# Value products of a pair's two heads issued together, alternating by key chunk, in a two-block attention network

## The reference

```python
# stick-breaking, 16 heads of 64 (first block, second layer)
z = q @ k.T * scale; suffix = reversed exclusive cumsum of log_sigmoid(-z)
wts = where(key < query, exp(log_sigmoid(z) + suffix), 0);  out = wts @ v
# second block, first layer: 8 global heads (2 key/value heads), 8 window heads (|rel| <= 128, bias, sink)
p = softmax(q @ k.T * scale [+ bias]);                      out = p @ v
# second block, second layer: 16 neighbourhood heads (8 rows x 16 columns of a 64-wide grid, bias)
p = softmax(where(colmask, q @ k.T * scale + bias, -inf));  out = p @ v
# both layers of the second block: 4 memory heads of 128 over 256 memory keys
```

## Time and profile before

| | |
|---|---|
| median of three runs | 2174.17 us |
| the profiled execution, its time | 2174.26 us |
| its span, first to last instruction | 2172.3 us |
| TensorE matmuls busy | 2086.6 us, 96% of the span |
| VectorE, ScalarE, GpSimd busy | 1155.4, 806.0, 131.6 us |
| mean granted TensorE clock | 0.981 |
| data moved | 173.78 MB, 80 GB/s on the mean |

### The profile page before, as it was taken

One profiled execution on the slowest core, in us unless ns is written; L12 is line 12 of the kernel. 1 busy time (PEld: TensorE's weight loads), 2 busy tenths in 40 slices (PEclk: granted clock), 3 DMA queues, 4 the chain that ended last, 5 costly groups with the idle time before them and its releaser, 6 DMA issues.

```text
span 2172.3 us, 26051 instructions
## 1 busy us (share of the span) xinstructions
PE 2086.6 (96%) x8940; PEld 1552.7 (71%) x8940; DVE 1155.4 (53%) x1991; ACT 806.0 (37%) x1402; POOL 131.6 (6%) x223
## 2 busy tenths in 40 slices
PE   6997999999999998999999998999998999999987
PEld 6875888888876665888888874555576866666766
DVE  6576544434555565544434555556744466666543
ACT  5365322222334444332222333534433333334331
POOL 1000000000000000000000000000003033332000
PEclk9999999999999999999999997999999999999998
DMA  6422223223321111222322320011122222222221
GB/s 217 145 79 67 90 96 104 97 89 96 106 69 58 49 48 39 89 97 97 111 82 97 104 71 20 29 64 47 56 74 74 85 68 69 69 68 56 83 73 68
DMA packets 48347, 173.78 MB, mean 80 GB/s; under 512 B 7345, under 2 KB 9409, under 8 KB 48017
## 3 DMA queue, kind: packets, MB, share of 16 engines
q1 hardware_dynamic: 41184, 160.45, 22.5%
q0 software_dynamic: 7088, 12.37, 2.3%
HBM read 168.58 MB, written 4.21 MB: 80 GB/s over the span
## 4 chain that ended last, share of the span: by engine, by line
PE 89%; DVE 6%; ACT 3%; issue 2%; DMA 1%; POOL 0%; DVEq 0%; ACTq 0%; SPq 0%; POOLq 0%
PE ps L366 24%; PE ps L368 23%; PE ps L367 23%; PE ps L458 7%; PE ps L486 7%; PE ps L466 3%; PE ps L544 1%; DVE Wl L1054 1%; ACT Wh L718 1%; DVE stat L1183 1%; DMA nmask<-in_nmask 1%; PE ps L435 0%; DVE scr L1180 0%; PE ps L401 0%; DMA Wr<-in_w 0%
## 5 line engine op out<-in xcount | busy, mean ns | idle before, releaser
L366 PE MATMUL ps<-Hh,Wh 128*128 128x512 f32 x1568 | 642.1, 410 | 0.0
L368 PE MATMUL ps<-Hh,Wl 128*128 128x512 f32 x1568 | 614.1, 392 | 0.0
L367 PE MATMUL ps<-Hl,Wh 128*128 128x512 f32 x1568 | 613.7, 391 | 0.0
L718 ACT ACTIVATE Wh<-Wr 128x1024 fp32r<-128x1024 f32 (+2 forms) x276 | 308.8, 1119 | 708.9 <-PE ps L368 696.2
L1054 DVE TENSOR_TENSOR Wl<-Wr,Wh 128x1024 fp32r<-128x1024 f32 (+2 forms) x276 | 359.3, 1302 | 240.1 <-ACT Wh L718 240.0
L366 PEld LDWEIGHTS ps<-Hh,Wh 128*128 128x128 f32 x1568 | 295.3, 188 | 142.2 <-issue 85.3
L368 PEld LDWEIGHTS ps<-Hh,Wl 128*128 128x128 f32 x1568 | 295.3, 188 | 64.5
L367 PEld LDWEIGHTS ps<-Hl,Wh 128*128 128x128 f32 x1568 | 295.7, 189 | 55.6 <-issue 0.7
L366 PE MATMUL ps<-Yh,Wh 128*128 128x512 f32 (+1 forms) x800 | 304.2, 380 | 30.9 <-DVE Yl L1084 16.5
L367 PE MATMUL ps<-Yl,Wh 128*128 128x512 f32 (+1 forms) x800 | 300.2, 375 | 0.0
L368 PE MATMUL ps<-Yh,Wl 128*128 128x512 f32 (+1 forms) x800 | 299.8, 375 | 0.0
(11 more groups left out here) (173 smaller groups left out, 1559.4 us busy)
## 6 DMA issues: line engine op xcount, KB each, us to landing
Wr<-in_w SPq DMA_DIRECT2D x228, 512.0 KB, 3.4
Wr<-in_w SPq DMA_DIRECT2D x32, 768.0 KB, 4.2
Wr<-in_w SPq DMA_DIRECT2D x16, 640.0 KB, 3.9
scr<-in_rpb POOLq DMA_DIRECT2D x128, 24.0 KB, 2.0
X<-in_x SPq DMA_DIRECT2D x1, 2048.0 KB, 13.6
scr<-in_wri POOLq DMA_DIRECT2D x4, 512.0 KB, 3.9
out_t<-X SPq DMA_DIRECT2D x8, 256.0 KB, 2.1
scr<-d_rel POOLq DMA_DIRECT2D x8, 192.0 KB, 3.3
```

What stands on the lines that cost most here:

```text
L366: pe.matmul(bank[:, 0:n], hi, rh[:, k, :], start=(k == 0), stop=False)
L367: pe.matmul(bank[:, 0:n], hi, rl[:, k, :], start=False, stop=False)
L368: return pe.matmul(bank[:, 0:n], lo, rh[:, k, :], start=False, stop=(k == kc - 1))
L718: act.activation(Wh[:, slot, 0:kc * P], Wr[:, slot, 0:kc * P], ACT.Copy).then_inc(w_hi, 1)
```

## The change

`values` is left to the memory heads. A new `values_pair` takes both heads of a pair: it goes over the key chunks, and within a chunk over the two heads, so that the products alternate between the two halves of `ps[6]`. It is called once for each pair, where head 1's visit stood; the call at step 6 is gone. It waits once for `t_pt`, `v_ok` and `yt_ok`. `t_av` is counted up by each head's last product, as before. In the gqa part the wait for `xf_ok` (the final norm of the first block has read `ps[6]`) moves from step 6 of pair 0 to step 2 of pair 1. No other engine's program changes.

```diff
--- before.py
+++ after.py
@@ -466,25 +466,30 @@
                     mm = pe.transpose(ps[4 + j % 2][:, n * P:(n + 1) * P], Pb[:, j % 4, n * P:(n + 1) * P], ident[:, :])
                 mm.then_inc(t_t, 1)
 
-            def values(kind, g, par, h, o, grp, v_need):
+            def values(g, par, h, o):
 
                 pe.wait_ge(t_pt, g + 1)
-                wait(pe, v_ok, v_need)
-                if h == 0 or kind == MEMA:
-                    wait(pe, yt_ok, o)
-                cs = range(2) if kind == MEMA else range(4)
-                for c in cs:
+                wait(pe, yt_ok, o)
+                m = 2 * par + h
+                for c in range(2):
+                    mm = pe.matmul(ps[6][:, :], memVa[:, c, m * P:(m + 1) * P], PT[:, h, c * S:(c + 1) * S],
+                                   start=(c == 0), stop=(c == 1), skip_group_check=True)
+                mm.then_inc(t_av, 1)
+
+            def values_pair(kind, g, par, o, grp, v_need):
+
+                pe.wait_ge(t_pt, g + 1)
+                pe.wait_ge(v_ok, v_need)
+                wait(pe, yt_ok, o)
+                for c in range(4):
                     q0, q1 = query_range(kind, c)
-                    rhs = PT[:, h, c * S + q0:c * S + q1]
-                    if kind == MEMA:
-                        m = 2 * par + h
-                        lhs, out = memVa[:, c, m * P:(m + 1) * P], ps[6][:, :]
-                    else:
+                    for h in range(2):
                         vb, off = {STICK: (par, h), NBR: (par, h), GQA: (0, grp), WIN: (1, grp)}[kind]
-                        lhs = Vn[:, vb, c * P + 64 * off:c * P + 64 * off + 64]
-                        out = ps[6][64 * h:64 * h + 64, q0:q1]
-                    mm = pe.matmul(out, lhs, rhs, start=(c == 0), stop=(c == cs[-1]), skip_group_check=True)
-                mm.then_inc(t_av, 1)
+                        mm = pe.matmul(ps[6][64 * h:64 * h + 64, q0:q1],
+                                       Vn[:, vb, c * P + 64 * off:c * P + 64 * off + 64], PT[:, h, c * S + q0:c * S + q1],
+                                       start=(c == 0), stop=(c == 3), skip_group_check=True)
+                        if c == 3:
+                            mm.then_inc(t_av, 1)
 
             def pump(j, nu, u0, t0, slot0):
 
@@ -580,9 +585,7 @@
                         if not (first and j < 2):
                             turn(kind, g - 2, (j - 2) % 8)
                         if j == 2 and not first:
-                            values(kind, g - 3, 1 - par, 1, i + (o0 - 1), 0, i + nv0)
-                        if j == 6:
-                            values(kind, g - 3, par, 0, i + o0, 0, i + (nv0 + 1))
+                            values_pair(kind, g - 3, 1 - par, i + (o0 - 1), 0, i + nv0)
                 pair(0, 0, True, False)
                 with pe.Fori(0, 3) as it:
                     pair(2 * it + 1, 1, False, False)
@@ -591,7 +594,7 @@
                 g = g0 + 64
                 turn(kind, g - 2, 6)
                 turn(kind, g - 1, 7)
-                values(kind, g - 1, 1, 1, o0 + 7, 0, nv0 + 8)
+                values_pair(kind, g - 1, 1, o0 + 7, 0, nv0 + 8)
 
             def mem_heads(seg, name, first_q):
                 plain_units(name, first_q, 4)
@@ -608,10 +611,10 @@
                             turn(MEMA, g - 2, (j - 2) % 8)
                         if j in (2, 6) and g - 3 >= g0:
                             hd = 2 * i + (j - 6) // 4
-                            values(MEMA, g - 3, hd // 2, hd % 2, OUT0[seg] + hd, 0, 0)
+                            values(g - 3, hd // 2, hd % 2, OUT0[seg] + hd)
                 turn(MEMA, g0 + 14, 6)
                 turn(MEMA, g0 + 15, 7)
-                values(MEMA, g0 + 15, 1, 1, OUT0[seg] + 3, 0, 0)
+                values(g0 + 15, 1, 1, OUT0[seg] + 3)
 
             pairs8("stick", STICK, "sb_qkv", 3, 8)
             out_proj("sb_out", KD, Y0["sb"])
@@ -689,15 +692,13 @@
                     if i < 3 and j == 6:
                         swap_halves(i + 2)
                     if j == 2 and i > 0:
-                        values(GQA if i <= 4 else WIN, g - 3, (i - 1) % 2, 1, o - 1, ((i - 1) % 4) // 2, 17)
-                    if i == 0 and j == 6:
+                        values_pair(GQA if i <= 4 else WIN, g - 3, (i - 1) % 2, o - 1, ((i - 1) % 4) // 2, 17 if i <= 4 else 18)
+                    if i == 1 and j == 2:
                         pe.wait_ge(xf_ok, KD)
-                    if j == 6:
-                        values(kind, g - 3, i % 2, 0, o, (i % 4) // 2, 17 if i < 4 else 18)
             g = STEP0["mem0"]
             turn(WIN, g - 2, 6)
             turn(WIN, g - 1, 7)
-            values(WIN, g - 1, 1, 1, OUT0["gqa"] + 7, 1, 18)
+            values_pair(WIN, g - 1, 1, OUT0["gqa"] + 7, 1, 18)
             mem_heads("mem0", "even_in", 20)
             out_proj("even_out", MIXC, Y0["even"])
```

## The result

The changed kernel takes 2116.62 us (median of 4 runs, 2116.08 to 2117.08) against 2173.88 us before (median of 4 runs), a ratio of 0.9739 (95% interval 0.9722 to 0.9756): 57 us less, where 40 were forecast, and below the range (2122 to 2175). One run of before, 2361.81 us, fell in a slower state and is left out of the ratio. The profiled execution has a span of 2114.8 us, 57.5 less than before.

The account below looks back on a forecast made before the run. TensorE was taken as the bound, its matmuls filling 96% of the span. 2174.3 less 3.8 for visits saved, less 38.2 for overlap, plus 2.4 given back made 2134.7, forecast as 2134 us; range 2122 to 2175.

Parts of the forecast that it names:

- nine slots of sixteen passes: Joint value visit: only one head's low pass overlaps the other's high pass; gqa 3.84 us instead of 6.83.
- the bare weight load: Joint value visit: each change of head starts its slot 0.05 us later, seven times, 0.37 us a visit.
- the alternation: Value products of two heads overlapping on two array halves: 38.2 us less over all stick, gqa, window and neighbourhood pairs.
- the 3.8 of visits saved: One value visit fewer in each pair: 24 visits at 0.16 us, 3.8 us less.
- Rival A: Value visits: overlap with the weight loads hidden too, 9 us more gained, 2125 us; chance 18%.
- R: Rule from the follow-ups, not predicted: a pass starts when its half is free and at most three passes wait ahead.
- B: Value visits: no overlap, only the saved visits remain, 2171 us; chance not stated separately.
- C: Value visits: each change of half costs 0.15 us, 25 us on top of B, 2196 us; chance 8%.
- The new wait: ScalarE's copy_t at step 2 waits for head 0's last product; 1.8 us of slack left, costed at nothing.
- The give-back: VectorE waits in window pairs and smaller gains in last stick, window and neighbourhood pairs: 2.4 us back.
- the 5 us that I had named as the sign of being wrong: Window stretch: VectorE's waits growing past 5 us would show the give-back wrong; they were 3.8 us before.

Follow-up runs that it names:

- all four orders: Changed kernel (heads alternating, 2116.62 us) and three reorderings of its value products: head by head 2148.19 us, two chunks per head 2118.19, three chunks then the fourth 2132.85.
- Same half: Changed kernel with head 1's value products also written to rows 0 to 63 of the bank, head 0's half; 2174.07 us.
- Three by three: Changed kernel with value products ordered three chunks of head 0, three of head 1, then the fourth of each; 2132.85 us.
- the best of each: Changed kernel with heads interleaved by step in stick and window pairs, only scores 3 and 4 issued together in gqa and neighbourhood; 2081.77 us.
- head by head: Changed kernel's joint visit with head 0's four value products first and head 1's four behind them; 2148.19 us.

## Why the prediction was wrong

**The step that failed** is "the order of issue still holds: high and low pass of one product use the same half and follow each other, but the low pass of one head and the high pass of the other can run together", which made nine slots of sixteen passes. I took the order in which instructions stand for the order in which they start. In the trace a pass that waits for its half does not hold up one for the other half, so there are eight slots and both heads start together. That is 0.43 us a gqa visit, 0.43 a stick visit (2.57 to 2.13) and 0.32 a neighbourhood or window visit, 9 us in all.

**The second term mis-sized** is the bare weight load. I carried 0.05 us per change of head over from visits with a single half, seven times a visit, 0.37 us; measured is 0.007 us once, since the two halves' loads start 5 to 7 ns apart, each beside the matmul in front of it on its own half. That is 9 us more. Together the alternation gave 20 x 2.13 + 4 x 3.42 = 56.3 us where I had 38.2; with the 3.8 of visits saved that is 60.1, where 57.3 were measured. Rival A had the loads right and the slots wrong (2125), and so no case of mine reached the time. The packing rule of the Trainium skill ("TensorE: Matmul & The Clock Gate", packing small matmuls), tiles starting some 4 ns apart, was nearer than my sum: the trace has 7. The same section says that matmuls start and end strictly in the order of the program, which is what my failed step amounts to; here head 1's high pass (1877.50) starts before head 0's low pass (1877.76), and the visits of all four orders fit R. Its rule that weight loads overlap running matmuls only where the row group differs does not hold here either: loads of both halves, all 128 rows each, run while both stream. (The section's part on the mechanism allows one more case, a load into the background weight buffer; no run here shows which buffer a load goes to.)

**B and C** are refuted: the visits of full pairs take 2.30 and 3.58 us, not 4.4 and 7.0, and no gap of 0.15 stands at a change of half. "Same half" is B made true, and came out at 2174, not 2171: the joint visit alone was worth nothing on the whole.

**The new wait costs nothing**, as forecast. In the neighbourhood visit ScalarE's copy, its rounding, VectorE's subtraction, and the unit that needs it (answering to the earlier trace rows):

```profile
1879.98 0.38 ACT L809 ACTIVATE scr<-ps 128x256 f32<-128x256 f32 x1 [3.41 <-PE ps L488]
1880.26 1.05 ACT L719 ACTIVATE Wh<-Wr 128x1024 fp32r<-128x1024 f32 x1
1881.34 1.23 DVE L1055 TENSOR_TENSOR Wl<-Wr,Wh 128x1024 fp32r<-128x1024 f32 x1 [5.00 <-ACT Wh L719]
...
1884.33 0.19 PEld L366 LDWEIGHTS ps<-Hh,Wh 128*128 128x128 f32 x1 [0.33 <-issue]
```

Ready at 1882.57, begun at 1884.33: 1.76 us of slack, 1.8 forecast; and no turn in the full neighbourhood pairs waits. From visit to visit these pairs take 34.46 us (1877.56 to 1912.02).

**The give-back was mis-sized as well, and hidden by luck.** 2.4 us were forecast, and 60.1 - 57.3 = 2.8 looks like it. By stretches it is not so. The table follows single matmuls of the weight units (in the fourth line a score) that stand in both programs:

| reached | before, us | now, us | earlier by |
|---|---|---|---|
| ahead of the stick pairs | 604.24 | 604.98 | -0.7 |
| behind them | 954.61 | 937.65 | 17.0 |
| further on, ahead of the second block | 1253.81 | 1236.85 | 17.0 |
| ahead of the first gqa visit | 1331.15 | 1310.98 | 20.2 |
| behind the window pairs | 1621.29 | 1579.43 | 41.9 |
| ahead of the neighbourhood pairs | 1762.64 | 1720.15 | 42.5 |
| behind them | 2042.09 | 1984.43 | 57.7 |

The stick pairs gave 17.7 us, gqa and window pairs 21.7 and neighbourhood pairs 15.2, together 54.6, where the visits alone (8 x 2.29, 4 x 3.58 + 4 x 2.29, 8 x 2.29) make 60.1. So 5.5 us were given back. Of what came in outside, 3.2 us lie ahead of the first gqa visit, where both kernels issue the same instructions: the clock was granted at 0.70 over 52 us before, at 0.79 over 49 us now.

```profile
1283.00:1335.00 52.00, 40.39 (x136) 26.64 (x135) 25.83 (x50) 10.13 (x17) 0.51 (x1) 0.70 0.10 31
...
1266.00:1315.00 49.00, 36.93 (x137) 24.75 (x135) 25.84 (x50) 10.17 (x18) 0.51 (x1) 0.79 0.11 33
```

"Three by three" and "the best of each" have 0.70 over the 52 us of the same steps, "same half" 0.79 over 49, so it is the single execution that differs and not the change. How much of it is in the medians, no run here shows.

What was given back has two parts. One is waits of the turns for VectorE, in the window stretch and in the last neighbourhood pair, after:

```profile
PE ps L466 <- DVE scr L1206: 5.0, 6, 2.2
...
PE ps L466 <- DVE scr L1206: 3.1, 3, 1.6
```

The same steps had 3.8 us in four waits and 1.8 in three before. So the window waits rose by 1.2 us (the 5 us that I had named as the sign of being wrong are just reached), and those of the last neighbourhood pair by 1.3. A full window pair gained 1.84 us where a neighbourhood pair gained 2.25 and a stick pair 2.30: of the 0.45 missing, 0.30 is a new wait of the turn of step 2.

The other part my sum put at nothing, the clock in the last pairs. With few weight units in them TensorE has idle time, and the granted clock falls to the 1.2 GHz level in places: the last stick pair has TensorE busy 17.9 of 23 us at a clock of 0.72 now (831:854), 20.6 of 26 at 0.80 before (846:872). The very last neighbourhood visit, before and now:

```profile
2016.61 2.37 PE ps L486 x8
...
1957.40 3.90 PE ps L488 x16
```

It takes 1.5 us more for slots that are the same in length and number at one clock: its first passes of 384 columns start 0.64 us apart (single records), where they start 0.32 apart at the 2.4 GHz level. Of the ten profiles with a joint visit nine have this visit at the lower level at least in part, that of "head by head" and that of before have not; why it falls just there is argued from the idle time and not shown. With the 1.3 us of waits and 6 x 0.04 in the full pairs this accounts for the 3.1 us that the neighbourhood pairs gave back.

## What to carry to other kernels

Where the output or the contraction of a product is 64 wide, issue it next to one on the other half of the array: here two such products cost what one did (visits of 2.30 and 3.58 us with eight passes and with sixteen). They need not alternate strictly: runs of two float32 products (four passes) of one half cost 0.05 us a visit, runs of three or four 0.9 and 1.8 us in gqa. Before pairing, look at who frees the bank or buffer of the second product, since the partner is wanted a step earlier: interleaved gqa pairs went from 30.8 to 34.5 us by it. And check a forecast stretch by stretch, with the granted clock of each, before its total is called right.

## What the hardware showed that I had not expected

- Two streams on different halves start 5 to 14 ns apart, some 0.06 us in the orders where one half's first load of a run stood bare, and each keeps its full rate (0.43 us for 512 columns), column halves and row halves alike; on the same half visits take 4.45 and 7.01 us.
- TensorE starts passes out of program order when their halves differ, past up to three waiting passes and, in four orders of issue, never past more: visits of 3.58, 3.63, 4.49 and 5.35 us in gqa.
